# First norm of a two-layer trunk: gain and bias as columns behind the transposition, and the square root at both ends on ScalarE

## The chip, the cores and the metric

The kernel runs on one core of a Trainium2 chip. The metric is the device time of one execution in microseconds (us); lower is better. TensorE (PE) multiplies matrices, VectorE (DVE), ScalarE (ACT) and GpSimd (POOL) work elementwise, and SyncE (SP) issues nearly all transfers. The engines run their own streams and meet at semaphores.

## The reference

The input is 256 tokens of width 1024 in float32. It is normalised first, and then two layers follow, each a mixer and a feed-forward part, each with a residual and another norm. Only the first and the last norm are touched by the change.

```
def _layer_norm(x, g, b):
    mu = mean(x, -1); var = mean((x - mu)**2, -1)
    return (x - mu) * rsqrt(var + 1e-5) * g + b

x = _layer_norm(x, ln_in_g, ln_in_b)
for l in range(2):
    mix = mixer(x, w_in[l], ...)          # starts with x @ w_in[l], 1024 x 6662
    x = _layer_norm(alpha * x + mix, ln1_g[l], ln1_b[l])
    ffn = swiglu(x, w_gate[l], w_up[l], w_down[l])
    x = _layer_norm(alpha * x + ffn, ln2_g[l], ln2_b[l])
```

## The kernel before

The 256 tokens are two tiles of 128 rows, `x[0]` and `x[1]`, of eight blocks of 128 columns each. `write_plan` writes one list of steps, and every engine walks it and does its own part of each step, so the order on an engine is the order of the list.

Weights arrive in pieces of up to 128x2048 in three `raw` buffers. ScalarE copies each to `w_hi` (step `hi`), VectorE subtracts to get `w_lo` (step `lo`), and TensorE multiplies in three products (L1438). SyncE may load the next piece into a `raw` buffer when the `lo` step of its last content is done.

The very first 512 columns of `w_in` go another way, since they need no splitting. They come in four quarters (`first_raw`, two blocks of rows each) and are multiplied in plain float32 (step `first_mm`, L1418: two records of TensorE for each product). The start runs so:

- TensorE works on zeros first (step `warm`, L1386), then spreads gain and bias, loaded as four rows, over all partitions of four banks (`spread_rows`, L1396), then does three more `warm` products.
- VectorE takes the statistics of a tile (L1317, L1319). GpSimd raises variance + 1e-5 to the power -0.5 (L946). VectorE corrects that root by one Newton step (L1337, L1340), and applies mean, gain, root and bias to `x` (L1327, L1347, L1350).
- TensorE transposes the blocks of `x` into a bank (step `turn_rows`, L1408), ScalarE copies the bank to `merged` (L1084), and TensorE multiplies that with `first_raw`. Later ScalarE and VectorE split `merged` into the two parts that all later pieces use (step `split_rows`, L1089, L1360).
- When tile 0 has its 512 columns, ScalarE copies the bank to `stages` (L1013), and TensorE transposes that (`turn_qk`, L1491) between the second and the third quarter of tile 1. Then come the pieces of the split kind (L1438).

At the end VectorE sums the last bank into `x` (L1278), ScalarE squares (L1094), GpSimd makes the root in two instructions (L953, L955), VectorE corrects it and scales (L1298, L1301, L1366), and SyncE stores the result.

## Time and profile before

| | |
|---|---|
| median of 3 runs | 831.04 us (830.87 to 831.71) |
| the profiled execution's own time | 831.25 us |
| its span in the profile | 829.5 us |
| TensorE busy | 819.2 us (99%) |
| VectorE, ScalarE, GpSimd busy | 535.7 us (65%), 435.9 us (53%), 55.4 us (7%) |
| chain that ended last | TensorE 95% |

The span runs from the first to the last recorded instruction; the execution's own time holds 1.75 us around it. Busy shares are means over the whole span, and the change touches the first 50 us and the last 10 us, so those stretches are read by themselves.

### The profile page before, as it was taken

Reading aid. Unit: us, or ns where it says so; the run is one execution under the profiler, and the core shown is the slowest. Engines: PE = TensorE matmul, PEld = TensorE weight load, DVE = VectorE, ACT = ScalarE, POOL = GpSimd, SP = SyncE. Lnnn points to the kernel's source line nnn. Section 1 sums busy time; section 2 is a strip of 40 time slices with the busy share of each in tenths; the row PEclk is TensorE's granted clock in tenths of the full one; section 3 lists DMA queues with packets and bytes.
Section 4 is the critical chain, followed back from the end, with each engine's and each line's share of the span. In section 5 each row is a group of like instructions: output and inputs, shape, how many; then the busy total and the mean of one; then the engine's idle time right before and its main releaser. Section 6 shows DMA issues by size and latency. Waiting matters only on the chain.

```text
span 829.5 us, 11237 instructions
## 1 busy us (share of the span) xinstructions
PE 819.2 (99%) x4305; PEld 684.4 (83%) x4305; DVE 535.7 (65%) x783; ACT 435.9 (53%) x622; POOL 55.4 (7%) x105
## 2 busy tenths in 40 slices
PE   9999999999999999999999999999999999999996
PEld 5888888888888888888889788878888888888885
DVE  7655656475776667566767656564686767576764
ACT  4667767654455344434448667666445544435431
POOL 0022230000000000000000414100000000000000
PEclk9999999999999999999999999999999999999999
DMA  8854443566448655654437543437754675656401
GB/s 296 273 192 140 140 141 127 179 227 216 139 152 303 206 185 171 216 190 152 153 110 251 177 151 113 144 103 250 243 190 149 207 252 165 224 169 202 169 37 51
DMA packets 93500, 148.33 MB, mean 179 GB/s; under 512 B 3460, under 2 KB 54916, under 8 KB 93448
## 3 DMA queue, kind: packets, MB, share of 16 engines
q1 hardware_dynamic: 93448, 147.62, 54.2%
q8 instruction: 35, 0.57, 0.3%
q14 instruction: 17, 0.14, 0.0%
HBM read 146.56 MB, written 1.05 MB: 178 GB/s over the span
## 4 chain that ended last, share of the span: by engine, by line
PE 95%; DVE 1%; DMA 1%; issue 1%; ACT 1%; SPq 1%; POOL 0%; POOLq 0%; DVEq 0%; ACTq 0%
PE bank L1438 62%; PE bank L1464 16%; PE bank L1467 8%; PE bank L1572 1%; PE bank L1562 1%; PE bank L1550 1%; PE bank L1481 1%; DMA raw<-in_w_in 1%; PE bank L1526 1%; PE bank L1491 1%; PE bank L1418 1%; DVE w_lo L1137 0%; DVE x L1278 0%; SPq L855 0%; SPq L851 0%
## 5 line engine op out<-in xcount | busy, mean ns | idle before, releaser
L1137 DVE TENSOR_TENSOR w_lo<-raw,w_hi 128x2048 fp32r<-128x2048 f32 (+5 forms) x182 | 310.1, 1714 | 94.3 <-ACT w_hi L990 93.9
L1438 PE MATMUL bank<-w_hi,act_parts 128*128 128x512 f32 (+2 forms) x1120 | 349.9, 384 | 0.7 <-DVE w_lo L1137 0.6
L990 ACT CAST w_hi<-raw 128x2048 fp32r<-128x2048 f32 (+3 forms) x140 | 253.5, 1812 | 104.9 <-PE bank L1467 56.8
L1438 PEld LDWEIGHTS bank<-w_hi,act_parts 128*128 128x128 f32 x1120 | 207.6, 188 | 39.7 <-issue 3.0
L1438 PE MATMUL bank<-w_lo,act_parts 128*128 128x512 f32 (+2 forms) x560 | 211.4, 378 | 0.0
L1464 PE MATMUL bank<-act_parts,w_hi 128*128 128x512 f32 x576 | 140.4, 391 | 0.0
L1464 PEld LDWEIGHTS bank<-act_parts,w_hi 128*128 128x128 f32 x576 | 105.7, 188 | 20.4
L1438 PEld LDWEIGHTS bank<-w_lo,act_parts 128*128 128x128 f32 x560 | 105.4, 188 | 16.9 <-issue 0.2
L1438 PE MATMUL bank<-w_hi,y_hi 128*128 128x512 f32 x240 | 94.9, 395 | 0.0
L1438 PE MATMUL bank<-w_lo,y_hi 128*128 128x512 f32 x240 | 93.6, 390 | 0.0
L1438 PE MATMUL bank<-w_hi,y_lo 128*128 128x512 f32 x240 | 93.5, 390 | 0.0
L1255 DVE TENSOR_REDUCE act_fns<-bank 128x256 f32<-128x512 f32 x72 | 47.9, 686 | 50.0 <-PE bank L1464 49.8
L1467 PEld LDWEIGHTS bank<-act_parts,w_lo 128*128 128x128 f32 x576 | 76.2, 191 | 4.2
L1467 PE MATMUL bank<-act_parts,w_lo 128*128 128x256 f32 x576 | 77.5, 282 | 0.0
L1438 PEld LDWEIGHTS bank<-w_hi,y_lo 128*128 128x128 f32 x240 | 45.0, 188 | 9.7
L1438 PEld LDWEIGHTS bank<-w_hi,y_hi 128*128 128x128 f32 x240 | 45.1, 188 | 9.1 <-issue 0.3
L1438 PEld LDWEIGHTS bank<-w_lo,y_hi 128*128 128x128 f32 x240 | 45.2, 188 | 8.4
L1105 ACT ACTIVATE act_fns<-act_fns 128x256 f32<-128x256 f32 x36 | 15.1, 418 | 70.2 <-DVE act_fns L1255 70.2
L1049 ACT ACTIVATE shared<-shared,neg_max 128x128 f32<-128x128 f32 (+3 forms) x64 | 33.7, 528 | 18.7 <-DVE neg_max L1206 13.4
L953 POOL TENSOR_SCALAR var_eps<-square_sum 128x1 f32<-128x1 f32 x8 | 1.5, 191 | 584.2 <-ACT prob_t_squares L1094 584.2
L1068 ACT ACTIVATE shared<-shared,rdenom 128x128 f32<-128x128 f32 (+1 forms) x64 | 25.6, 448 | 27.7 <-DVE rdenom L1226 27.7
L1152 DVE TENSOR_TENSOR qk_parts<-bank,qk_parts 128x512 fp32r<-128x512 f32 (+1 forms) x24 | 14.4, 600 | 32.4 <-ACT qk_parts L1019 32.4
(135 smaller groups left out, 564.7 us busy)
## 6 DMA issues: line engine op xcount, KB each, us to landing
raw<-in_w_in SPq DMA_DIRECT2D x42, 1024.0 KB, 5.1
raw<-in_w_gate SPq DMA_DIRECT2D x44, 512.0 KB, 4.0
raw<-in_w_up SPq DMA_DIRECT2D x44, 512.0 KB, 5.1
raw<-in_w_down SPq DMA_DIRECT2D x22, 1024.0 KB, 4.9
raw<-in_w_o SPq DMA_DIRECT2D x8, 1024.0 KB, 5.1
raw<-in_w_in SPq DMA_DIRECT2D x8, 768.0 KB, 4.6
raw<-in_w_pa SPq DMA_DIRECT2D x4, 768.0 KB, 4.5
raw<-in_w_pc SPq DMA_DIRECT2D x4, 768.0 KB, 4.5
```

Source lines behind the costliest of these rows:

```text
L990: act.copy(weights(w_hi, i, HI_SLOTS), weights(raw, i, RAW_SLOTS)).then_inc(hi_done, 1)
L1049: act.activation(pr, pr, ACT.Exp, bias=neg_max[:, slot:slot + 1], scale=-1.0, accum_out=denom[:, slot:slot + 1]).then_inc(exp_done, 1)
L1068: ins = act.activation(pr, pr, ACT.Identity, scale=rdenom[:, slot:slot + 1])
L1105: act.activation(a[:, 0:256], a[:, 0:256], ACT.Silu).then_inc(silu_done, 1)
L1137: dve.tensor_tensor(weights(w_lo, i, HI_SLOTS)[:, cols], weights(raw, i, RAW_SLOTS)[:, cols], weights(w_hi, i, HI_SLOTS)[:, cols].bitcast( ...
L1152: dve.tensor_tensor(qk_lo[ev["g"] % 2][:, pairs, cols], group_view(bank[b], ev["np"], P), qk_hi[ev["g"] % 2][:, pairs, cols].bitcast(F32), ...
L1255: dve.tensor_reduce(a[:, part * SEQ:(part + 1) * SEQ], bank[b][:, :].rearrange("p (h n) -> p n h", h=2), mybir.AxisListType.X, ALU.add).th ...
L1418: ins = pe.matmul(bank[use[0]][:, :], merged[t][:, at_k * P:(at_k + 1) * P], first_raw[q][:, k, :], start=at_k == 0, stop=at_k == KT - 1)
L1438: ins = pe.matmul(bank[use[0]][:, 0:width], a, w[:, k, c0:c0 + width], start=start and k == 0 and p == 0, stop=stop and k == nk - 1 and p ...
L1464: ins = pe.matmul(out[:, :], wh[:, k, cols], act_parts[:, at_k, :, :], start=begins and k == 0, stop=ends and k == 3)
L1467: ins = pe.matmul(out[:, 0:SEQ], wl[:, k, cols], hi["act"][:, at_k, :], start=begins and k == 0, stop=ends and k == 3)
L1481: ins = pe.transpose(out[:, k * P:(k + 1) * P], source(src, buf, k0 + k, t), ident)
```

## The change

Gain and bias of the first norm are loaded as 2 x 8 columns beside the identity matrix (`FIRST_COLS`), so that after the transposition, where the channels lie on the partitions, ScalarE puts them on as scale and bias of its copy out of the bank. One instruction of 128 columns for each block takes the place of one for a whole bank. VectorE only subtracts the mean and multiplies by the root. `spread_rows` goes away, and TensorE's work on zeros becomes 20 products in one go. The first half of `x[0]` and the identity are loaded from ScalarE's queue. The first and the second block of tile 0 have a bank each, and TensorE multiplies the first before it transposes the third and fourth. The root of tile 0 is ScalarE's `Abs_reciprocal_sqrt`. Since the rows of `x` now lack gain and bias, both are loaded to all partitions later, and GpSimd completes the rows (`complete_rows`) before the first scores. In the last norm ScalarE makes the root itself. The pieces of the diff stand in the order plan, SyncE, GpSimd, ScalarE, VectorE.

```
-WARM = (10, 3)
+WARM = 20
...
-    plan.append(("warm", WARM[0]))
-    plan.append(("spread_rows", spread_rows))
-    plan.append(("warm", WARM[1]))
-    plan.append(("first_norm", 0, spread_rows))
-    turn_rows(0, (0, 2), (2, 2))
-    plan.append(("first_norm", 1, spread_rows))
+    plan.append(("warm", WARM))
+    plan.append(("first_norm", 0))
+    turn_rows(0, (0, 1), (1, 1, bank(1)))
+    plan.append(("first_norm", 1))
...
-            first_mm(0, 0, use0[0])
+            first_mm(0, 0, use0[0], (0,))
+            turn_rows(0, (2, 2))
+            first_mm(0, 0, use0[0], (1,))
             turn_rows(0, (4, 4))
             split_rows(0)
             first_mm(0, 1, use0[0])
-            split_hi()
             first_mm(0, 2, use0[0])
             turn_rows(1, (0, 4))
+            split_hi()
             first_mm(0, 3, use0[0])
...
+                    if (layer, c, half, t) == (0, 2, 1, 0):
+                        plan.append(("complete_rows",))
...
-            sp.dma_start(norm_rows, d["norms"]).then_inc(norms_loaded, 16)
-            load_x(0)
+            load_x(0, 1)
             load_first(0)
-            sp.dma_start(tables[:, 0:P], d["tables"][:, 0:P]).then_inc(ident_loaded, 16)
             load_first(1)
-            load_x(1)
+            load_x(1, 0, 1)
...
+                    if i == 2 * RAW_SLOTS - 1:
+                        sp.wait_ge(filled[first_chunk[0]], first_chunk[1])
+                        broadcast_gain_bias(0)
...
+                elif step[0] == "complete_rows":
+                    pool.wait_ge(gb_loaded, 32)
+                    for t in range(TT):
+                        for b, n in first_turns[t]:
+                            pool.wait_ge(drained[b], n)
+                        link(pool.tensor_tensor(x[t][:, :], x[t][:, :], gain_bias[:, 0, :], ALU.mult))
+                        pool.tensor_tensor(x[t][:, :], x[t][:, :], gain_bias[:, 1, :], ALU.add).then_inc(rows_complete, 1)
...
+            act.dma_start(x[0][:, 0:NW], d["x"][0:P, 0:NW]).then_inc(x_loaded[0][0], 16)
+            act.dma_start(tables[:, 0:FIRST_COLS], d["norms"]).then_inc(ident_loaded, 16)
...
+                elif kind == "first_norm" and step[1] == 0:
+                    act.wait_ge(eps_ready, 1)
+                    link(act.activation(early_root[:, :], eps[:, :], ACT.Abs_reciprocal_sqrt))
+                    act.wait_ge(first_var, 1)
+                    act.activation(rstd[:, 0:1], mean_var[:, 0, 1:2], ACT.Abs_reciprocal_sqrt,
+                                   bias=eps[:, :]).then_inc(first_root, 1)
...
-                    act.copy(merged[t][:, k0 * P:(k0 + nk) * P], bank[b][:, 0:nk * P]).then_inc(drained[b], 1)
+                    for k in range(nk):
+                        at_k = k0 + k
+                        ins = act.activation(merged[t][:, at_k * P:(at_k + 1) * P], bank[b][:, k * P:(k + 1) * P],
+                                             ACT.Identity, scale=gain_cols[:, at_k:at_k + 1],
+                                             bias=bias_cols[:, at_k:at_k + 1])
+                    ins.then_inc(drained[b], 1)
...
+                        if step[3] == 2 * DEPTH:
+                            act.wait_ge(squares_ready, means)
+                            act.activation(rstd[:, t:t + 1], square_sum[:, t:t + 1], ACT.Abs_reciprocal_sqrt, bias=eps[:, :],
+                                           scale=1.0 / D_MODEL).then_inc(root_ready, 1)
...
+                    if u["u"] == 0:
+                        dve.wait_ge(rows_complete, TT)
...
+                    def normalise(c0, c1):
+                        return dve.tensor_scalar(x[t][:, c0:c1], x[t][:, c0:c1], mean_var[:, t, 0:1], rstd[:, one],
+                                                 ALU.subtract, ALU.mult)
```

The order of instructions shows the change at three places. First, ScalarE's stream at the start of the kernel, before; `merged` is the transposed tile, `act_parts` its split form, `w_hi` a weight piece, `stages` the first 512 columns of tile 0, and the brackets hold the semaphores waited for.

```order
L1084 ACT_TABLE_LOAD
L1084 COPY merged<-bank 128x256 [waits filled7]
L1084 COPY merged<-bank 128x256 [waits filled6]
L1084 COPY merged<-bank 128x512 [waits filled7]
L1089 CAST act_parts<-merged 128x8x128 [waits drained7,drained6]
L990 CAST w_hi<-raw 128x1536 [waits raw_full0]
L1084 COPY merged<-bank 128x512 [waits filled6]
L1084 COPY merged<-bank 128x512 [waits filled7]
L990 CAST w_hi<-raw 128x1536 [waits raw_full1]
L1013 COPY stages<-bank 128x512 [waits filled0]
L1089 CAST act_parts<-merged 128x8x128 [waits drained7,drained6]
```

The same place in the changed kernel, from its first copies out of a bank to the copy to `stages`:

```order
L1110 ACTIVATE merged<-bank,tables 128x128 [waits ident_loaded,filled6]
L1110 ACTIVATE merged<-bank,tables 128x128
L1110 ACTIVATE merged<-bank,tables 128x128 [waits ident_loaded,filled7]
L1110 ACTIVATE merged<-bank,tables 128x128 x3
L1118 CAST act_parts<-merged 128x8x128 [waits drained6,drained7,drained1]
L1110 ACTIVATE merged<-bank,tables 128x128 [waits ident_loaded,filled6]
L1110 ACTIVATE merged<-bank,tables 128x128 x3
L1007 CAST w_hi<-raw 128x1536 [waits raw_full0]
L1110 ACTIVATE merged<-bank,tables 128x128 [waits ident_loaded,filled7]
L1110 ACTIVATE merged<-bank,tables 128x128 x3
L1007 CAST w_hi<-raw 128x1536 [waits raw_full1]
L1030 COPY stages<-bank 128x512 [waits filled0]
```

Each copy of 512 columns has become four of 128, and the first weight piece has moved from ahead of both copies of tile 1 to between them; the copy to `stages` still stands behind two weight pieces and both sets of copies of tile 1.

Second, TensorE's stream before the first split pieces, before; `tables` holds the identity, `shared` and `act_fns` the quarters of the first weights:

```order
L1386 MATMUL bank<-logf_lo,logf_hi 128x256 [waits ident_loaded]
L1386 MATMUL bank<-logf_lo,logf_hi 128x256 x2
L1408 MATMUL bank<-tables,x 128x128 [waits first_quarter]
L1408 MATMUL bank<-tables,x 128x128
L1408 MATMUL bank<-tables,x 128x128 [waits x_ready]
L1408 MATMUL bank<-tables,x 128x128
L1418 MATMUL bank<-shared,merged 128x512 [waits first_loaded0,drained7]
L1418 MATMUL bank<-shared,merged 128x512
L1408 MATMUL bank<-tables,x 128x128 [waits drained7,x_ready]
```

And the same place now, from its very start:

```order
L1405 MATMUL bank<-logf_lo,logf_hi 128x256 [waits logf_zeroed]
L1405 MATMUL bank<-logf_lo,logf_hi 128x256 x19
L1416 MATMUL bank<-tables,x 128x128 [waits first_quarter,ident_loaded] x2
L1426 MATMUL bank<-shared,merged 128x512 [waits drained7,first_loaded0]
L1416 MATMUL bank<-tables,x 128x128 [waits x_ready,ident_loaded]
L1416 MATMUL bank<-tables,x 128x128
L1426 MATMUL bank<-shared,merged 128x512 [waits drained1,first_loaded0]
L1416 MATMUL bank<-tables,x 128x128 [waits drained7,x_ready,ident_loaded]
L1416 MATMUL bank<-tables,x 128x128 x3
```

The eight products that spread gain and bias are gone, the work on zeros stands in one go ahead of everything, and the first product needs only the first block.

Third, ScalarE's last instructions, before and then now; `rstd` is the root, `prob_t_squares` the squares:

```order
L1105 ACTIVATE act_fns<-act_fns 128x256 [waits drained6]
L1107 CAST y_hi<-act_fns 128x256 [waits hid_done]
L1094 ACTIVATE prob_t_squares,square_sum<-x,neg_mean 128x1024 [waits mean_ready] x2
```

```order
L1138 ACTIVATE act_fns<-act_fns 128x256 [waits drained6]
L1140 CAST y_hi<-act_fns 128x256 [waits hid_done]
L1143 ACT_TABLE_LOAD
L1143 ACTIVATE early_root<-eps 128x1 [waits eps_ready]
L1123 ACTIVATE prob_t_squares,square_sum<-x,neg_mean 128x1024 [waits mean_ready,act_own]
L1127 ACTIVATE rstd<-square_sum,eps 128x1 [waits squares_ready]
L1123 ACTIVATE prob_t_squares,square_sum<-x,neg_mean 128x1024 [waits mean_ready]
L1127 ACTIVATE rstd<-square_sum,eps 128x1 [waits squares_ready]
```

A table load and a root on a constant have come behind the last feed-forward copy, and each square is followed by the root.

## Rows read from the trace of the kernel before

**Rows 1.** Chain of waits, 0 to 30 us: start us, us, what.
```profile
0.72 0.37 SPq L857
...
1.15 0.36 SPq L851
...
17.45 3.70 PE bank L1418 x8
21.15 0.44 PE bank L1491 x4
21.59 3.44 PE bank L1418 x8
25.02 4.19 PE bank L1438 x24
```

**Rows 2.** Stretches: us, busy time of each engine, TensorE clock, DMA share, GB/s.
```profile
8.70:24.40 15.70, 15.40 (x47) 7.59 (x48) 13.27 (x20) 9.53 (x13) 0.55 (x1) 1.00 0.98 337
24.40:820.00 795.60, 794.82 (x4227) 670.06 (x4226) 511.12 (x736) 423.46 (x607) 52.78 (x94) 1.00 0.54 177
```

**Rows 3.** Timeline of TensorE, 0 to 26 us.
```profile
1.33 2.50 PE L1386 MATMUL bank<-logf_lo,logf_hi 128*128 128x256 f32 x10 [1.33 <-POOL logf_lo L916]
...
6.83 0.63 PE L1396 MATMUL bank<-w_lo,w_hi 128*128 128x512 f32 x1
7.39 0.70 PE L1386 MATMUL bank<-logf_lo,logf_hi 128*128 128x256 f32 x3
...
8.77 1.98 PE L1418 MATMUL bank<-shared,merged 128*128 128x512 f32 x4 [0.24 <-ACT merged L1084]
```

**Rows 4.** Timeline of VectorE, 0 to 22 us.
```profile
4.03 1.34 DVE L1317 BATCH_NORM_STATS2 stats<-x 128x6 f32<-128x512 f32 x2 [0.47 <-DMA x<-in_x]
5.40 0.21 DVE L1319 BATCH_NORM_AGGREGATE mean_var<-stats 128x2 f32<-128x12 f32 x1
...
6.64 0.22 DVE L1337 SCALAR_TENSOR_TENSOR newton<-rstd,half_var 128x1 f32<-128x1 f32 x1
6.89 0.16 DVE L1340 SCALAR_TENSOR_TENSOR rstd<-newton,rstd 128x1 f32<-128x1 f32 x1
7.09 0.48 DVE L1347 SCALAR_TENSOR_TENSOR x<-x,rstd,bank 128x256 f32<-128x256 f32 x1
```

**Rows 5.** Timeline of ScalarE, 0 to 22 us.
```profile
15.44 1.47 ACT L990 CAST w_hi<-raw 128x1536 fp32r<-128x1536 f32 x1 [2.46 <-DMA raw<-in_w_in]
16.82 1.07 ACT L1084 COPY merged<-bank 128x512 f32<-128x512 f32 x2
17.77 1.48 ACT L990 CAST w_hi<-raw 128x1536 fp32r<-128x1536 f32 x1
19.14 0.60 ACT L1013 COPY stages<-bank 128x512 f32<-128x512 f32 x1
```

**Rows 6.** Groups of ScalarE by form: count, busy us, mean ns, idle before.
```profile
L1068 ACT ACTIVATE shared<-shared,rdenom 128x128 f32<-128x128 f32 x32 | 11.1, 395 | 19.1 <-DVE rdenom L1226 19.1
...
L1028 ACT ACT_TABLE_LOAD x1 | 1.3, 1283 | 0.0
...
L1013 ACT COPY values<-bank 128x128 f32<-128x128 f32 x4 | 1.1, 286 | 0.0
...
L1028 ACT ACTIVATE f_exp<-f_neg_abs 128x12 f32<-128x12 f32 x2 | 0.4, 212 | 0.6 <-DVE f_neg_abs L1163 0.6
```

**Rows 7.** Timeline of ScalarE, 52 to 66 us.
```profile
59.98 0.69 ACT L1068 ACTIVATE shared<-shared,rdenom 128x128 f32<-128x128 f32 x2 [1.97 <-DVE rdenom L1226]
```

**Rows 8.** Timeline of the end, GpSimd, then VectorE, 820 to 829.5 us.
```profile
824.18 0.19 POOL L953 TENSOR_SCALAR var_eps<-square_sum 128x1 f32<-128x1 f32 x1 [7.33 <-ACT prob_t_squares L1094]
...
825.11 0.22 DVE L1298 SCALAR_TENSOR_TENSOR newton<-rstd,half_var 128x1 f32<-128x1 f32 x1 [0.77 <-POOL rstd L955]
```

**Rows 9.** Groups of GpSimd by form.
```profile
L963 POOL TENSOR_TENSOR shared<-shared 128x512 f32<-128x512 f32 x4 | 6.9, 1726 | 0.3
```

**Rows 10.** Timeline of VectorE, 51 to 55 us.
```profile
53.52 0.49 DVE L1191 TENSOR_TENSOR shared<-bank,tables 128x128 f32<-128x128 f32 x2
```

More of the change, by code:

```diff
@@ L277, in turn_rows @@
     def turn_rows(t, *parts):
-        for k0, nk in parts:
-            use = aux_bank()
+        for k0, nk, *other in parts:
+            use = other[0] if other else aux_bank()
             turned.update({("first", t, k): use for k in range(k0, k0 + nk)})
@@ L826, in group_view @@
             return ap[:, 0:groups * width].rearrange("p (g k) -> p g k", g=groups)
+        first_chunk = next(step[3] for step in PLAN if step[0] == "first_mm" and step[1:3] == (TT - 1, QUARTERS - 1))
         first_turns = [[step[4] for step in PLAN if step[0] == "turn_rows" and step[1] == t] for t in range(TT)]
@@ L947, in _ @@
                                        ALU.pow).then_inc(first_root, 1)
-                elif step[0] == "statistics":
+                elif step[0] == "statistics" and step[3] < 2 * DEPTH:
                     for t, _ in step[1]:
@@ L1107, in _ @@
                     act.copy(hi["y"][:, 2 * (c % 3) + j, :], a[:, 256:512]).then_inc(hid_hi_done, 1)
+                    if turned_n == last_turned:
+                        act.wait_ge(eps_ready, 1)
+                        link(act.activation(early_root[:, :], eps[:, :], ACT.Abs_reciprocal_sqrt))
         @block.vector
@@ new lines, in _ @@
+                    if t:
+                        link(dve.bn_aggr(mean_var[:, t, :], stats[:, t, :, :]))
+                        dve.tensor_scalar(var_eps[:, one], mean_var[:, t, 1:2], LN_EPS, None,
+                                          ALU.add).then_inc(first_var, 1)
+                    else:
+                        dve.bn_aggr(mean_var[:, t, :], stats[:, t, :, :]).then_inc(first_var, 1)
+                        dve.wait_ge(first_var, 1)
+                    link(dve.tensor_scalar(half_var[:, one], mean_var[:, t, 1:2], LN_EPS, -0.5, ALU.add, ALU.mult))
@@ L1387, in _ @@
                                   start=True, stop=True)
-                elif kind == "spread_rows":
-                    pe.wait_ge(rows_hi_done, 1)
-                    pe.wait_ge(rows_lo_done, 1)
-                    for a, uses in enumerate(step[1]):
-                        for j, use in enumerate(uses):
-                            out, done = take(use)
-                            r = 2 * a + j
-                            for p, part in enumerate((rows_hi, rows_lo)):
-                                ins = pe.matmul(out[:, :], row_pick[:, r:r + 1].broadcast_to([P, P]), part,
-                                                start=p == 0, stop=p == 1)
-                            ins.then_inc(done, 1)
-                    pe.wait_ge(ident_loaded, 16)
                 elif kind == "turn_rows":
                     _, t, k0, nk, use = step
-                    if (t, k0) == (0, 0):
+                    pe.wait_ge(ident_loaded, 16)
+                    if t == 0 and k0 < 2:
                         pe.wait_ge(first_quarter, 1)
@@ L1410, in _ @@
                 elif kind == "first_mm":
-                    _, t, q, use, (b, n) = step
-                    pe.wait_ge(drained[b], n)
+                    _, t, q, use, rows = step
                     pe.wait_ge(first_loaded[q], 16)
-                    if q == 0:
-                        take(use)
-                    for k in range(2):
+                    for k in rows:
                         at_k = 2 * q + k
+                        if at_k == 0:
+                            take(use)
+                        pe.wait_ge(drained[rows[k][0]], rows[k][1])
                         ins = pe.matmul(bank[use[0]][:, :], merged[t][:, at_k * P:(at_k + 1) * P],
```

111 lines of the change are left out of this document (40 added, 71 removed).

## The prediction

> **What bounds the kernel now.** I read the busy time by stretches first. From 24.4 to 820 us TensorE is busy 794.82 of 795.60 us [rows 2], so nothing on the other engines is worth anything there unless it makes TensorE wait. From 8.7 to 24.4 us it is busy 15.40 of 15.70 us, but before 8.77 us it only works on zeros, spreads gain and bias and transposes [rows 3]. So the time is: when TensorE begins useful work, plus fixed work, plus its gaps up to 25 us, plus the tail behind its last product. The change can act in the first and the last of these, and in the gaps.
>
> In the chain of waits the point to watch is where the first split piece begins, at 25.02 us [rows 1]: from there on the stream is unchanged. Ahead of it stand the transposition of the first result (21.15 us) and four products of two records, 3.44 us, so one costs 0.86 us; four transposes cost 0.44 us.
>
> **The start, up to the first product.** VectorE begins the statistics at 4.03 us, having waited for the transfer of `x` [rows 4], which was issued at 1.15 us behind the four rows of gain and bias [rows 1]. Now both halves are issued at about 0.72 us from two queues. The first half alone would come 0.4 us sooner; but the two now share the transfer engines, and the statistics before ran over both halves in one go (1.34 us for two), so the second half was no wait. Bounds: 0.3 us sooner to 0.2 us later. I take no change. The aggregate ends at 5.61 us.
>
> ScalarE's root has no row. The nearest is a ScalarE instruction on 12 columns, 0.212 us; an operand read for each partition adds 0.395 - 0.286 = 0.11 us at 128 columns [rows 6]; so 0.32 us, from 5.66 to 5.98. Newton begins at 6.03 instead of 6.64 us; its two steps take 0.25 and 0.20 us [rows 4], and the first 256 columns begin at 6.48 us. They took 0.48 us with a second tensor; without it, between half of the streaming part saved (0.34) and nothing (0.48); I take 0.40: 6.88 us against 7.57. One block's transposition I put at 0.4 us with its pipeline (four take 0.44), one copy with scale and bias at 0.50 us (0.395 with one such operand, 0.11 for the second), wakes 0.1 us: the first product begins at 7.9 us instead of 8.77 [rows 3], some **0.85 us sooner**.
>
> **From the first product to the split pieces.** This is where I expect the gain to go. ScalarE now puts four instructions where one was. Two of 128 columns with one operand for each partition took 0.69 us together, 0.395 each alone, so they follow each other at 0.295 us [rows 6, 7]; with a second such operand 0.295 to 0.40 us. I take 0.39, for the second operand is read like the first. A bank then takes 3 x 0.39 + 0.49 = 1.66 us; before it was about 0.6, and two banks 1.07 us [rows 5]. At 0.295 it is 1.28 us.
>
> TensorE: product, two transposes, product, four transposes: 7.9 + 0.1 + 0.86 + 0.22 + 0.86 + 0.44 = 10.4 us. Two products end at 12.1 us; blocks 4 to 7 reach `merged` at 10.6 + 1.66 = 12.25, a wait of 0.15 us. Two more products, 14.0 us; transposes of tile 1, 14.45 us, in the bank at 14.6 us. Then product pairs, transposes and the first half of tile 1 bring TensorE to the transposition of `stages` at about 20.2 us by the chain's count, 0.95 us ahead of before (it also loses the gap it had before 17.45 us).
>
> ScalarE's stream decides whether `stages` is there. Before: piece 0 at 15.44 us, waiting for its transfer, both copies at 16.82, piece 1 at 17.77, `stages` from 19.14 to 19.74 us [rows 5]: 1.4 us before TensorE's 21.15. Now the four copies of tile 1 begin at 14.65, and piece 0 follows them at 16.2 us, no longer bound by its transfer. Then 1.38 us to the next copies, 4 x 0.39 = 1.56, piece 1 and 1.37 us, `stages` 0.60: 21.1 us. TensorE's transposition follows some 0.3 us later (wake, weights, pipeline), at 21.4 us instead of the 20.2 it could. The split pieces begin 0.44 + 3.44 us later, at 25.3 us, against 25.02: **0.3 us lost**, though the first product came 0.85 us sooner. With 0.295 us for each copy every number falls: copies from 14.45, piece 0 at 15.65, `stages` at 20.15, split pieces at 24.35: 0.7 us won. With 0.40 us it is 0.4 lost. These are the bounds of the term.
>
> The Trainium skill bears on this: "ScalarE: Activation LUTs", What ACT_TABLE_LOAD costs, says that each operand read for each partition adds some 93 ns and that instructions in a row overlap by as much. By its figures two operands give 0.386 us from one to the next, and the term would be the 0.3 us lost that I take; if the second operand is free, it would be 0.7 us won. The rows agree for one operand (0.295); none has two.
>
> **What else is added, and its cover.** The root needs a different activation table, so a load of 1.283 us [rows 6] comes before the exponential of the forget gate; the instruction waited 0.6 us for VectorE there, so the chain slips 0.7 us. It feeds a sum that TensorE reaches some 4 us after its input is ready, and ScalarE's next piece is not needed for several us: nothing. Gain and bias for all partitions are 1 MB more behind the sixth piece; at the 337 GB/s of rows 2 that is 3.1 us on the pieces behind. They are copied near 35 us and multiplied after 50 us: nothing, as long as the delay stays below about 8 us. GpSimd's four passes of 1024 columns: the nearest row is 512 columns in 1.726 us [rows 9], so up to 3.5 us each, 14 us, from about 35 to 49 us. VectorE waits for them in front of the first scores, at 53.52 us [rows 10]: hidden by 4 us. If that cover were gone, each us beyond would stop VectorE, the splits queued behind it, and then TensorE.
>
> **The end.** GpSimd wakes at 824.18 us, and VectorE gets the root at 825.11 us, having been idle 0.77 us [rows 8]. Now ScalarE goes on itself at about 824.2 us and takes 0.32 us; VectorE at 824.55 us: **0.55 us won** (0.45 to 0.65). The table load before it falls on an idle ScalarE.
>
> **Sum.** 0.3 us lost at the start, 0.55 won at the end: 0.25 us won, 831.25 to 831.0 us for the profiled execution. That execution lies 0.21 us over the median of the runs shown, 831.04, so I expect 830.8 us.
>
> **Rivals.**
> *A, the copies are cheap.* The second operand costs nothing; split pieces 0.7 us sooner, with the end 1.25 us: 829.8 us. With `x` 0.3 us sooner too, and a quick subtraction, 829.3. For it: scale and bias may be fetched together. Against it: the first operand cost 0.11 us.
> *B, TensorE's clock is still low at the first product* (the other side). Ten products of 256 columns took 2.50 us from 1.33 us on, three took 0.70 us at 7.39 us, and the products between, to 6.83 us, run at the slow pace too [rows 3]: the 1.2 GHz level held until about 7.4 us of nearly unbroken work, and it was at 2.4 GHz in time for 8.77 us. Now 20 products of about 0.22 us end at 5.8 us, and TensorE idles until 6.95 us. If the rise then comes at 11 us, half of 7.9 to 11 us is lost, 1.55 us, and slower transposes 0.1: 832.4 us. A rise at 13 us gives 833.4. From the point where the rise is later than about 8.5 us it cancels the gain. The Trainium skill, "TensorE: Matmul & The Clock Gate", The HAM clock gate, says that the low level is the default, that sustained activity ends it, and that the moment varies between executions of one kernel. By that rule some executions rise during the 20 products and some do not; one trace cannot show it.
> *C, the completed rows come late.* If a pass on GpSimd took over 4.6 us, the first scores would wait; at 6 us each that is 5.5 us on VectorE, of which perhaps 2 reach TensorE: 832.8 us or more. The rows give 3.5 us at most.
>
> **How the numbers follow.** The main case (830.3 to 831.4 us) gets 0.42, A 0.24, B 0.28, C 0.06. About 0.2%, 1.7 us, is what a measurement of this kernel can tell from no change: 829.4 to 832.7 us. A reaches below it with 0.15; B beyond it with 0.10 and C with 0.03. So faster 0.15, same 0.72, slower 0.13. The range leaves out the far ends of A and of B and C, 0.1 each: 829.2 to 832.8 us.
>
> **What the profile after would show.** The first product at 7.9 us and at most 0.5 us for one copy; four copies in 1.66 us (1.28 in A); TensorE waiting about 1.2 us for `stages` ahead of its transposition; the split pieces at 25.3 us; work on zeros and first products at either pace, which tells B; the first scores not waiting for GpSimd; VectorE's last correction waiting some 0.2 us for the root instead of 0.77. A start of the statistics more than 0.3 us from 4.03 us, or a wait of TensorE for weights behind 30 us, would show a step that I have not priced.

## The result and the profile after

The change made the kernel slower: 839.24 us median of 5 runs (838.25 to 840.04), against 830.87 us for the kernel before on the same chip (830.81 to 831.71). The ratio is 1.0096, with a 95% interval of 1.0085 to 1.0107. The profiled execution took 840.04 us with a span of 838.2 us, 8.7 us more than the span before.

The stretches of the kernel after stand below (us, busy time of each engine, granted TensorE clock, DMA share, GB/s):

```profile
8.70:25.50 16.80, 16.18 (x47) 7.86 (x46) 8.57 (x14) 12.13 (x22) 0.56 (x1) 0.90 0.72 244
25.50:60.00 34.50, 30.18 (x158) 26.66 (x157) 23.99 (x20) 21.19 (x30) 15.46 (x7) 0.91 0.71 243
60.00:820.00 760.00, 759.35 (x4031) 637.97 (x4030) 490.21 (x707) 404.14 (x578) 51.20 (x90) 1.00 0.54 175
```

From 60 us on TensorE is as full as in [rows 2]. Ahead of that it idles for 4.3 us between 25.5 and 60 us, where before it did not idle at all, and in both early stretches the mean clock is below full. TensorE's five longest waits in the kernel after (line, releaser: us in total, times, longest) name the place:

```profile
PE bank L1509 <- DVE logf_lo L1209: 4.3, 1, 4.3
PE bank L1416 <- DVE x L1358: 1.5, 1, 1.5
PE bank L1405 <- POOL logf_lo L921: 1.3, 1, 1.3
PE bank L1499 <- ACT stages L1030: 0.6, 1, 0.6
PE bank L1426 <- ACT merged L1110: 0.5, 1, 0.5
```

L1509 is the running sum of the forget gate's logarithms, a product of TensorE that needs VectorE's last result of the gate (`logf_lo`). GpSimd's timeline of the kernel after from 36 us on (start us, us) shows the four passes:

```profile
36.95 4.36 POOL L954 TENSOR_TENSOR x<-x,shared 128x1024 f32<-128x1024 f32 x1 [26.44 <-DVE qk_parts L1188]
41.38 2.40 POOL L955 TENSOR_TENSOR x<-x,shared 128x1024 f32<-128x1024 f32 x1
43.74 4.44 POOL L954 TENSOR_TENSOR x<-x,shared 128x1024 f32<-128x1024 f32 x1
48.26 3.22 POOL L955 TENSOR_TENSOR x<-x,shared 128x1024 f32<-128x1024 f32 x1
```

VectorE's timeline of the same stretch shows what it did beside them:

```profile
36.76 2.28 DVE L1173 TENSOR_TENSOR w_lo<-raw,w_hi 128x2048 fp32r<-128x2048 f32 x1
41.46 4.47 DVE L1173 TENSOR_TENSOR w_lo<-raw,w_hi 128x2048 fp32r<-128x2048 f32 x1 [2.42 <-ACT w_hi L1007]
45.85 0.41 DVE L1188 TENSOR_TENSOR qk_parts<-bank,qk_parts 128x256 fp32r<-128x256 f32 x1
46.19 3.08 DVE L1173 TENSOR_TENSOR w_lo<-raw,w_hi 128x1024 fp32r<-128x1024 f32 x1
49.19 2.33 DVE L1196 TENSOR_TENSOR f_in<-f_in,f_bias 128x12 f32<-128x12 f32 x1
51.55 0.17 DVE L1199 SCALAR_TENSOR_TENSOR f_neg_abs<-f_in 128x12 f32<-128x12 f32 x1
...
54.26 0.21 DVE L1209 TENSOR_TENSOR logf_lo<-neg_logf,logf_hi 128x48 fp32r<-128x48 f32 x1 [0.35 <-ACT logf_hi L1054]
```

The same subtraction of 2048 columns takes 2.28 us where it begins ahead of GpSimd's first pass, and 4.47 us beside a pass. An addition on 12 columns takes 2.33 us and ends at 51.52 us, just behind GpSimd's last pass (51.48 us). So `logf_lo` starts at 54.26 us, where before it started at 43.63 us.

Laid side by side, the two timelines look as if one engine stood while the other worked. The second pass ends at 43.78 us, and the subtraction begun at 41.46 us ends 2.15 us later; the third pass ends 2.25 us behind that, the subtraction of 1024 columns 1.09 us behind that, the fourth pass 2.21 us behind that, and the small addition 0.04 us behind the pass. Undisturbed, they take 2.29 us (subtraction), 2.40 us (the second pass), 1.22 us and 0.16 us. The first pass fits as well: it stood behind the subtraction begun at 36.76 us. The operation on `qk_parts`, which reads one of its two inputs out of a bank, took 0.41 us while the third pass ran, as in the kernel before (0.43 us).

The clock follows. These are slices of 2 us of the kernel after, with the same columns as above:

```profile
52.00:54.00 2.00, 0.00 (x0) 0.00 (x0) 0.35 (x2) 1.99 (x6) 0.00 (x0) 0.89 0.00 0
54.00:56.00 2.00, 1.48 (x5) 1.48 (x6) 1.34 (x2) 2.00 (x4) 0.00 (x0) 0.50 0.00 0
56.00:58.00 2.00, 2.00 (x6) 1.52 (x6) 1.87 (x1) 2.00 (x3) 0.00 (x0) 0.50 0.56 116
58.00:60.00 2.00, 2.00 (x6) 1.54 (x5) 1.93 (x4) 1.97 (x3) 1.08 (x3) 0.50 1.06 397
60.00:62.00 2.00, 2.00 (x16) 1.39 (x15) 1.97 (x2) 0.00 (x0) 2.00 (x1) 0.90 1.02 363
```

TensorE had been idle since 50.2 us; it resumes at 54.52 us at 1.2 GHz, does 6 records in a slice (56 to 60 us) where at 2.4 GHz it does 11 of this kind (42 to 48 us), and gets the full clock back just behind 60 us. Half of its busy time in the three slices at 0.50 and a tenth of the last are lost, 2.9 us. The Trainium skill, "TensorE: Matmul & The Clock Gate", HAM oscillation, says that idle gaps between bursts of products bring the low level back; these slices agree.

At the start the same happens once more. TensorE's timeline of the kernel after:

```profile
1.33 4.61 PE L1405 MATMUL bank<-logf_lo,logf_hi 128*128 128x256 f32 x20 [1.33 <-POOL logf_lo L921]
7.43 0.41 PE L1416 MATMUL bank<-tables,x 128*128 128x128 f32 x2 [1.50 <-DVE x L1358]
8.37 1.24 PE L1426 MATMUL bank<-shared,merged 128*128 128x512 f32 x2 [0.53 <-ACT merged L1110]
9.41 0.64 PE L1416 MATMUL bank<-tables,x 128*128 128x128 f32 x2
9.84 1.91 PE L1426 MATMUL bank<-shared,merged 128*128 128x512 f32 x2
```

ScalarE's timeline of the kernel after, with its root and the first pair of the new copies:

```profile
6.01 0.29 ACT L1102 ACTIVATE rstd<-mean_var,eps 128x1 f32<-128x1 f32 x1 [2.87 <-DVE mean_var L1353]
7.77 0.81 ACT L1110 ACTIVATE merged<-bank,tables 128x128 f32<-128x128 f32 x2 [1.47 <-PE bank L1416]
```

And VectorE's, which begins 0.35 us later than in [rows 4]:

```profile
4.38 1.29 DVE L1346 BATCH_NORM_STATS2 stats<-x 128x6 f32<-128x512 f32 x2 [4.38 <-DMA x<-in_x]
```

The first product's two records take 1.24 us, the second product's 1.91 us, although both have the same shape: the clock fell between them, behind the idle time from 5.94 to 7.43 us. The mean granted clock from 9.0 to 12.6 us was 0.53.

So the first split piece starts at 26.42 us instead of 24.46 us by TensorE's records (1.96 us). With 4.32 us of idle time and 2.9 us of low clock, less 0.57 us won at the end (shown below), this is 8.6 of the 8.7 us.

### The profile page after: what moved, and what is told of

The parts are those of the page before. It is cut to its first block, busy times and chain, and to the rows that moved or that the text cites. A ratio compares the mean times of both kernels' runs of the same rounds, so it can differ in the third digit from the quotient of the medians.

```text
span 838.2 us, 11253 instructions
## 1 busy us (share of the span) xinstructions
PE 822.2 (98%) x4304; PEld 686.3 (82%) x4304; DVE 536.3 (64%) x772; ACT 443.1 (53%) x640; POOL 68.1 (8%) x105
## 4 chain that ended last, share of the span: by engine, by line
PE 91%; DVE 3%; DMA 3%; ACT 2%; issue 1%; SPq 0%; POOL 0%; DVEq 0%; ACTq 0%
PE bank L1446 59%; PE bank L1472 16%; PE bank L1475 8%; PE bank L1580 1%; DVE w_lo L1173 1%; DMA raw<-in_w_in 1%; PE bank L1570 1%; PE bank L1426 1%; PE bank L1558 1%; PE bank L1534 1%; PE bank L1489 1%; PE bank L1499 1%; DMA raw<-in_w_up 1%; DMA x<-in_x 0%; ACT w_hi L1007 0%
## 5 line engine op out<-in xcount | busy, mean ns | idle before, releaser
L1173 DVE TENSOR_TENSOR w_lo<-raw,w_hi 128x2048 fp32r<-128x2048 f32 (+5 forms) x182 | 314.3, 1736 | 100.3 <-ACT w_hi L1007 100.0
L1188 DVE TENSOR_TENSOR qk_parts<-bank,qk_parts 128x512 fp32r<-128x512 f32 (+1 forms) x24 | 14.4, 600 | 29.5 <-ACT qk_parts L1036 29.5
```

Source lines behind the costliest of these rows:

```text
L1173: dve.tensor_tensor(weights(w_lo, i, HI_SLOTS)[:, cols], weights(raw, i, RAW_SLOTS)[:, cols], weights(w_hi, i, HI_SLOTS)[:, cols].bitcast( ...
L1188: dve.tensor_tensor(qk_lo[ev["g"] % 2][:, pairs, cols], group_view(bank[b], ev["np"], P), qk_hi[ev["g"] % 2][:, pairs, cols].bitcast(F32), ...
```

## The experiments

All medians are in us, beside runs of the kernel before on the same chip. The edits are cut to the lines that matter and moved to the left; `...` marks lines left out.

### The end alone

```
+if step[3] == 2 * DEPTH:                      # ScalarE, last norm, on the kernel before
+    act.wait_ge(squares_ready, means)
+    act.activation(rstd[:, t:t + 1], square_sum[:, t:t + 1], ACT.Abs_reciprocal_sqrt,
+                   bias=eps[:, :], scale=1.0 / D_MODEL).then_inc(root_ready, 1)
...
```

The table for this root is loaded early, as in the change, and GpSimd's two instructions for the last norm are left out.

> The kernel before, with one part of the change alone: the root of the last row tile's last norm is taken by ScalarE from its own sum of squares, its table loaded early. The prediction priced this at 0.55 us won. Compared with the kernel before (830.9): 830.3, ratio 0.9993 to 0.9994, and in the profile the Newton step waits some 0.2 us for ScalarE instead of 0.77 us for GpSimd. If the rest of the span between the profiles (8.7 us longer) hid a loss in the end too, this would be at or over the time of before.

Measured: 830.49 (11 runs) against 831.03 (27 runs), ratio 0.9993 (0.9984 to 1.0002). The medians differ by 0.54, as forecast, though the interval includes 1. The profile shows the step itself. VectorE's timeline at the end of this kernel:

```profile
824.33 0.22 DVE L1310 SCALAR_TENSOR_TENSOR newton<-rstd,half_var 128x1 f32<-128x1 f32 x1 [0.19 <-ACT rstd L1103]
```

The same place in the kernel after:

```profile
833.94 0.22 DVE L1336 SCALAR_TENSOR_TENSOR newton<-rstd,half_var 128x1 f32<-128x1 f32 x1 [0.20 <-ACT rstd L1127]
```

The wait is 0.19 us instead of 0.77 [rows 8]. This part works.

### Passes and loads taken out

```
-link(pool.tensor_tensor(x[t][:, :], x[t][:, :], gain_bias[:, 0, :], ALU.mult))
-pool.tensor_tensor(x[t][:, :], x[t][:, :], gain_bias[:, 1, :], ALU.add).then_inc(rows_complete, 1)
+pool.memset(pass_mark[:, t:t + 1], 0.0).then_inc(rows_complete, 1)
...
```

> The changed kernel with GpSimd's four passes (gain, then bias, on both row tiles, 128x1024 each) left out, so gain and bias are missing in the rows that the residual adds; the two broadcasts of gain and bias and SyncE's wait ahead of them stay. Theory 1, GpSimd's passes hold VectorE (its 2048 column subtraction took 4.47 instead of 2.29 us, a 128x12 addition 2.33 instead of 0.16), the forget gate's sum comes 4.3 us late and the idle TensorE loses its clock: 4.3 + 3.4 = 7.7 us come back, 831.5 (830.5 to 832.5), and no low clock behind 50 us. Theory 2, the broadcasts and the wait in SyncE's queue hold up the pieces (the casts waited 3.28, 2.62 and 0.90 us for them): 837 or more. Between the two (833 to 836): the 4.3 us come back and the clock stays low for another reason.

Measured: 832.72 (10 runs, 830.81 to 833.17), ratio 1.0017 (1.0008 to 1.0027). Removing four GpSimd instructions brings back 6.5 of the 8.4 us. The median is just above the range I gave (830.5 to 832.5): in the profile the clock at the start is low here too (below), and TensorE waits 0.9 us for `cum_row`, VectorE's next result of the gate. Transfers and SyncE's wait are untouched here, so by themselves they are not where the time went. No run has the passes without the loads in the changed kernel, so how much of the 6.5 us needs both is not shown.

```
-sp.wait_ge(filled[first_chunk[0]], first_chunk[1])
-broadcast_gain_bias(0)
...
```

> As the one before it, and without the two broadcasts for the first norm and SyncE's wait for the last first product too; the later norms' gain and bias are loaded as before. Theory 1: the transfers are covered, same time as with them within 0.3 us (about 831.5). Theory 2: all of the loss but the start's comes back only here, 831 to 832 while the kernel with the transfers stays at 837 or more. If both kernels gain a part, the difference of the two is the price of the transfers.

Measured: 832.45 (10 runs, 830.97 to 833.70), ratio 1.0015 (1.0006 to 1.0024): without the passes the broadcasts cost 0.3 us by the medians, which runs that spread over 2.4 and 2.7 us do not tell from nothing. But they are not without effect. `logf_lo` is ready at 45.25 us without them and at 48.80 us with them, and TensorE comes for it at 48.38 and 49.74 us. The spare time is 3.1 us without the broadcasts, 0.9 us with them (these two profiled runs differ in the start's clock as well, see below), and it was 4.2 us in the kernel before (43.84 to 48.09 us).

The runs fall in two groups: three without loads lie at 830.97 to 831.11, seven at 832.26 to 833.70. The profiled one was among the three. Its first stretches:

```profile
9.00:12.60 3.60, 3.60 (x14) 1.56 (x11) 2.30 (x8) 2.31 (x6) 0.56 (x1) 1.00 1.05 387
12.60:25.50 12.90, 12.29 (x39) 6.09 (x39) 7.68 (x7) 10.72 (x17) 0.20 (x2) 1.00 0.72 231
```

The first of them in the profiled run of the kernel with the loads, which took 832.79 us:

```profile
9.00:12.60 3.60, 3.60 (x12) 1.78 (x11) 2.29 (x8) 1.05 (x3) 0.56 (x1) 0.69 1.05 387
```

The clock at the start differs, 1.00 against 0.69, and the two groups of the kernel without loads lie 1.6 us apart (medians 831.07 and 832.67). Each run's mean granted clock goes the same way in the kernel without loads: 0.998 in the three quick runs, 0.995 to 0.997 in the seven others. Where in the run the clock was low is read from one profile of each kind; the next runs test it.

### TensorE kept at work until the transposition

```
-WARM = 20
+WARM = 28
```

> The changed kernel with 28 warm-up products instead of 20, so that TensorE is at work until the first transpositions instead of idle from 5.94 to 7.43 us. Theory 3: that idle stretch is what takes the clock down between 9.19 and 12.6 us, and half of this stretch is lost by it: 1.7 us come back, 837.5 (837.0 to 838.2). Rival: the low stretch comes from the chain of short transpositions and products behind 7.43 us (each waits for a copy), which stay: 839.2, within 0.3 us of the changed kernel, with the clock low at 9 to 12 us as before. A third way: the warm-up ends too late and holds the transpositions up, 839.5 or more.

Measured: 836.66 (5 runs, 836.36 to 837.39), ratio 1.0069 (1.0056 to 1.0082), 2.6 us better than the kernel after. TensorE now idles 0.3 us ahead of its transposition, and the clock from 9 to 12.6 us is 1.00. I had forecast 1.7 us (837.0 to 838.2), too little: the first split piece came 1.33 us sooner (25.09 us), and the wait for `logf_lo` fell from 4.3 to 3.4 us as well.

To test the two groups, the same was done to the kernel without passes and loads:

> The changed kernel without passes, broadcasts and SyncE's wait (gain and bias are missing in the rows that the residual adds), with 28 warm-up products. It is what the prediction summed: start, copies, end. Theory 3, the start's clock is what keeps the kernel without passes and loads at 832.5 in 7 of 10 executions and lets it at 831.0 in 3: all executions at 830.6 to 831.2. If the low executions stay (832.4 and more), the idle time ahead of the transpositions is not what lowers the clock. The prediction's own sum, 830.8, should be met within 0.3.

Measured: 830.95 (11 runs, 830.77 to 831.22), ratio 0.9995 (0.9986 to 1.0003). The group above 832 us is gone in all 11 runs. With 8 more products on zeros, this kernel holds the terms that my sum counted (start, copies, end) and of those that it put at nothing only the table load, and it comes within 0.15 us of the 830.8 forecast.

### The passes alone, in the kernel before

Nothing else of the change is in this kernel; the passes work on the gate's buffers, which are idle then, and neither on `x` nor on the loaded gain and bias. ScalarE waits for their end before it writes there.

```
+elif step[0] == "idle_passes":                # GpSimd, on the kernel before
...
+    pool.wait_ge(hi_done, 6)
+    for op in (ALU.mult, ALU.add, ALU.mult, ALU.add):
+        link(pool.tensor_tensor(act_fns[:, 0:1024], act_fns[:, 0:1024], act_fns[:, 1024:2048], op))
...
```

> The kernel before with GpSimd's four passes of 128x1024 and two inputs added to it alone, on idle memory (the gate's buffers, which nobody reads until they are overwritten), from some 34 us on; no other part of the change. The same output is computed. Theory 1 (GpSimd's passes hold VectorE wherever VectorE subtracts beside them): the 2048 column subtraction behind 34 us takes 3.5 to 4.5 instead of 2.29 us, the forget gate's last VectorE result comes 3 to 7 us later than 43.63, and since TensorE wants it only at 48.0, 0 to 3 us are lost; with the clock falling in addition up to 5: 831.0 to 836, likeliest 832.5. Rival: it is the changed kernel's later start and later pieces alone that made the passes dear; then 831.0 and subtractions of 2.29 us.

Measured: 836.45 (5 runs, 836.11 to 836.53), ratio 1.0061 (1.0048 to 1.0075): 5.3 us lost by four instructions on an engine that is 7% busy, and above the range that I gave (831.0 to 836). GpSimd's timeline in this kernel:

```profile
33.85 14.56 POOL L952 TENSOR_TENSOR act_fns<-act_fns 128x1024 f32<-128x1024 f32 x4 [21.56 <-ACT w_hi L1001]
```

VectorE's beside it:

```profile
34.76 8.06 DVE L1149 TENSOR_TENSOR w_lo<-raw,w_hi 128x2048 fp32r<-128x2048 f32 x2
...
43.08 3.09 DVE L1149 TENSOR_TENSOR w_lo<-raw,w_hi 128x1024 fp32r<-128x1024 f32 x1
46.09 2.35 DVE L1172 TENSOR_TENSOR f_in<-f_in,f_bias 128x12 f32<-128x12 f32 x1
48.48 0.17 DVE L1175 SCALAR_TENSOR_TENSOR f_neg_abs<-f_in 128x12 f32<-128x12 f32 x1
```

And TensorE's, where it waits for the forget gate:

```profile
51.45 0.59 PE L1513 MATMUL bank<-upper_r,logf_hi 128*128 128x384 f32 x1 [3.25 <-DVE logf_lo L1185]
```

Two subtractions take 8.06 us (before: 4.48 us), and `f_neg_abs` starts 7.55 us later than before (40.93 us). Less the 4.2 us of spare time, that is 3.35 us, near TensorE's wait of 3.25 us. The clock is 0.50 from 52 to 54 us and 0.75 from 54 to 56 us, which costs 1.5 us more. The rival, that only the late start made the passes dear, falls.

### What in a pass does it

Each pass in four of 256 columns:

```
+for c0 in range(0, D_MODEL, 256):
+    part = slice(c0, c0 + 256)
+    pool.tensor_tensor(x[t][:, part], x[t][:, part], gain_bias[:, 0, part], ALU.mult).then_inc(pool_own, 1)
...
```

> The changed kernel, each of GpSimd's four passes cut into four of 256 columns; the same is computed. Theory 1a, VectorE's instruction is held until GpSimd's present instruction ends (the 128x12 addition took 2.33 us and ended with GpSimd's pass): the small addition is held for a quarter pass at most, 0.2 to 1.1 us, while the 2048 column subtractions are as slow as before, and 1 to 1.5 us of the 8.4 us come back, 837.7 to 838.3. Theory 1b, the two share the memory by halves as long as both have work, so only the sum of the work counts: the small addition is again some 2 us, 839.2 within 0.5. Theory 2 (transfers), already weak: no change.

Measured: 836.25 (4 runs, 835.92 to 838.58), ratio 1.0067 (1.0054 to 1.0081), 3.0 us better than the kernel after. VectorE's timeline:

```profile
43.65 1.68 DVE L1184 TENSOR_TENSOR w_lo<-raw,w_hi 128x1024 fp32r<-128x1024 f32 x1
45.26 0.70 DVE L1207 TENSOR_TENSOR f_in<-f_in,f_bias 128x12 f32<-128x12 f32 x1
45.99 0.65 DVE L1210 SCALAR_TENSOR_TENSOR f_neg_abs<-f_in 128x12 f32<-128x12 f32 x1
...
48.76 0.67 DVE L1215 TENSOR_SCALAR neg_logf<-neg_logf 128x12 f32<-128x12 f32 x1
```

The small addition is held 0.5 us instead of 2.2 us, so it is held for one GpSimd instruction, not for a share of the work. Theory 1b falls. The last line has one input only and is held as well (0.17 us undisturbed). The forecast of 1a (837.7 to 838.3) missed that the big subtractions gain too (1.68 us instead of 3.08 for 1024 columns): now it is the passes that stretch, four quarters to 5.84 us beside VectorE, against 2.82 us where VectorE is mostly idle. TensorE's wait for `logf_lo` shrinks from 4.3 to 0.2 us, but one of 2.1 us for `cum_row` (VectorE's next result of the gate) follows.

The passes with one input:

```
+link(pool.tensor_scalar(x[t][:, :], x[t][:, :], 1.0, None, ALU.mult))
+pool.tensor_scalar(x[t][:, :], x[t][:, :], 0.0, None, ALU.add).then_inc(rows_complete, 1)
```

> The changed kernel with GpSimd's four passes as operations of one input and a constant (times 1, plus 0) in place of two inputs, so gain and bias are missing in the rows that the residual adds. Theory 1, it is the reading of GpSimd's two inputs that holds VectorE: with one input the passes are shorter (under 2 us) and VectorE's subtractions go back to 2.29 us or near, 832 to 834. Rival: any large instruction of GpSimd beside a VectorE instruction of two inputs holds it; then 836 or more, and the subtractions still take over 3 us.

Measured: 834.79 (4 runs, 832.35 to 836.55), ratio 1.0042 (1.0025 to 1.0058). The median lies between the two forecasts, and the runs spread over 4 us; the profiled one is the quickest. In it VectorE is nearly free (one subtraction of 3.01 us, the others 2.29, the small addition 0.17 us), but GpSimd's passes still take 2.8 to 3.7 us. By the medians one input is better than two by 4.45 us. Whether VectorE is released in the slower executions too is not seen.

### The rows completed by VectorE

Except for the one marked below, these kernels compute everything. They have 28 warm-up products, and VectorE makes the two passes over each tile.

```
+def complete_rows(t):                         # VectorE
+    dve.wait_ge(gb_loaded, 32)
+    link(dve.tensor_tensor(x[t][:, :], x[t][:, :], gain_bias[:, 0, :], ALU.mult))
+    link(dve.tensor_tensor(x[t][:, :], x[t][:, :], gain_bias[:, 1, :], ALU.add))
```

> The changed kernel with 28 warm-up products, and with the rows completed by VectorE instead of GpSimd, in its idle time: row tile 0 ahead of the last projection block's subtractions, row tile 1 while ScalarE takes the forget gate's exponential and logarithm (1.88 us idle). Two operations of two inputs and 1024 columns each, 1.22 us by the nearest row (1024 column subtraction), 4.9 us in all against 2.3 + 1.9 us of idle time in these places. Theory 1: TensorE waits for the forget gate's sum no more than 1 us, the clock stays full, 831.0 to 832.3. If the placement of any 5 us of work there costs the clock as well, 835 or more, and the fault would be the completion's place, not its engine.

Measured: 833.89 (5 runs, 833.52 to 835.74), ratio 1.0036 (1.0023 to 1.0049), 1.6 us worse than the upper end I gave, since I had allowed TensorE one wait of up to 1 us, and there were two. TensorE's waits in this kernel:

```profile
PE bank L1536 <- DVE cum_row L1219: 1.6, 1, 1.6
PE bank L1407 <- POOL logf_lo L921: 1.3, 1, 1.3
PE bank L1511 <- DVE logf_lo L1213: 1.3, 1, 1.3
```

The clock stays at 1.00 throughout, in spite of these two waits. An operation takes 1.22 us here, against 2.40 to 4.44 us on GpSimd.

```
+elif kind == "turn_rows" and step[1:3] == (1, 4):   # VectorE instead of ScalarE
...
+        ins = dve.tensor_scalar(merged[t][:, at_k * P:(at_k + 1) * P],
+                                bank[b][:, (at_k - k0) * P:(at_k - k0 + 1) * P],
+                                gain_cols[:, at_k:at_k + 1], bias_cols[:, at_k:at_k + 1],
+                                ALU.mult, ALU.add)
```

> As the one before it, and the last four transposed blocks of row tile 1 are put on by VectorE (gain as multiplier, bias as addend, from the bank) instead of ScalarE's four copies of 0.39 us. The prediction's step: ScalarE's copies make the stages late, 0.3 us lost against before. If right, TensorE's wait of 0.6 us for the stages goes and this kernel is 0.5 to 0.7 us faster than the one before it, 830.4 to 831.7. If the stages are held by something else than the copies (the cast of the weights ahead of them), the two are equal within 0.2 us.

Measured: 833.24 (11 runs, 832.42 to 835.67), ratio 1.0029 (1.0020 to 1.0039), 0.65 us better than the one before it, as forecast, but above the range I gave (830.4 to 831.7), since the two waits for the gate stay (0.9 and 1.6 us). The runs of the two kernels overlap. Without passes and loads, so with gain and bias missing in the rows that the residual adds, the same edit gives the clean comparison:

> As the one before it (no passes, no broadcasts, 28 warm-up products; gain and bias missing in the residual's rows), with the last four transposed blocks of row tile 1 put on by VectorE. The prediction's term of 0.3 us lost by ScalarE's copies: TensorE's wait of 0.6 us for the stages goes, 829.9 to 830.4. If it isn't the copies, 830.8 as without them.

Measured: 830.24 (11 runs, 830.11 to 830.43), ratio 0.9988 (0.9980 to 0.9997), 0.71 us below the 830.95 of the kernel with ScalarE's copies, and no run of one lies among those of the other. VectorE's four take 1.37 us, and TensorE's wait for `stages` is gone.

Last, with everything computed again, row tile 0 is completed one step earlier in the order, in VectorE's wait for a cast:

```
-if (layer, c, half, t) == (0, 2, 1, 0):
+if (layer, c, half, t) == (0, 2, 0, TT - 1):
```

> The version with the rows completed by VectorE and the shared copies (833.2), with row tile 0's completion moved ahead of the 2048 column subtraction at 38.8 us, into the 2.1 us that VectorE waits there for ScalarE's cast; row tile 1's stays in the wait for the exponential and logarithm. All is computed. Of TensorE's waits for the forget gate's sum and its row (0.9 + 1.6 us) 2.1 us should go: 831.1, range 830.5 to 832.0. If the broadcasts land too late for this place (behind 37 us), the subtraction behind it comes later and it stays at 832.5 or more.

Measured: 830.98 (11 runs, 830.41 to 831.70), ratio 0.9997 (0.9989 to 1.0006), where I had forecast 831.1. VectorE's timeline:

```profile
36.48 1.22 DVE L1163 TENSOR_TENSOR x<-x,shared 128x1024 f32<-128x1024 f32 x1
37.73 1.23 DVE L1164 TENSOR_TENSOR x<-x,shared 128x1024 f32<-128x1024 f32 x1
39.05 2.29 DVE L1175 TENSOR_TENSOR w_lo<-raw,w_hi 128x2048 fp32r<-128x2048 f32 x1
```

Both passes fit into the idle time, and the subtraction starts only 0.3 us later than in the version that completed tile 0 behind it (38.77 us). This computes the whole reference, is 8.3 us faster than the kernel after and cannot be told from the kernel before. No version that computes everything beat the kernel before by more than the measurement can tell; the best of them is the end alone, 830.49. Only the incomplete kernel with shared copies has an interval below 1. In the last kernel TensorE still waits 0.7 us for `cum_row`.

## Why the prediction was wrong

I forecast 830.8 us (829.2 to 832.8) and gave slower by over 0.2% a chance of 0.13. It took 839.24 us.

**The step that failed** is the one on GpSimd: "up to 3.5 us each, 14 us, from about 35 to 49 us ... hidden by 4 us". The size came out nearly right by luck: four passes, 14.4 us, from 36.95 to 51.48 us. But a pass that was not held up took 2.40 us; the three others stretched to 3.22 to 4.44 us because they too stood behind VectorE. VectorE's first scores never waited for them. What failed is that I priced them only by who waits for their result. I did not ask whose instructions they run beside. The passes held three of VectorE's instructions up by 2.2, 1.9 and 2.2 us (4.47 for 2.29, 3.08 for 1.22, 2.33 for 0.16), the forget gate came 5.7 us later than without them (54.26 against 48.59 us), and TensorE idled 4.3 us and then ran 2.9 us short at 1.2 GHz. In the kernel before the passes alone cost 5.3 us, in the kernel after 6.5 us by the medians with and without them. With the passes out, the median is 832.72 us, inside the stated range; they alone took the kernel out of it. My rival C had the right instructions and the wrong mechanism: it let them be late, and asked for 4.6 us each.

The profile before had a row that warned of it. It stands in GpSimd's timeline there, beside VectorE's subtraction of 51.20 to 53.49 us:

```profile
51.72 2.09 POOL L937 TENSOR_TENSOR rope_cos<-stages,tables 128x128 f32<-128x128 f32 x1 [39.33 <-ACT stages L1013]
53.89 0.46 POOL L938 TENSOR_TENSOR rope_sin<-stages,tables 128x128 f32<-128x128 f32 x1
```

Two instructions of one shape: 2.09 us beside a two-input subtraction, 0.46 us when it has ended. Here GpSimd is the one that is held; with a large GpSimd instruction ahead it is VectorE. The Trainium skill, "GPSIMD Engine Reference", Specifications, states that GpSimd shares its memory interfaces with VectorE and that they contend where VectorE's instruction has two inputs in that memory. By that rule VectorE's subtractions for `w_lo`, which have two such inputs, were all suspects. The trace of before agrees, and so do the subtractions and the additions held beside passes with two inputs, and `qk_parts`, with one of its inputs in a bank, which was not held. The passes with one input mostly left the subtractions alone in the one profile, and an instruction of VectorE with one input was held beside quartered passes; the sentence on two inputs decides neither.

**The second failed step** is in rival B, which I gave 0.28: the place and the price were right, the reading was not. I took the clock to be low at first ("the 1.2 GHz level held until about 7.4 us"). The rows do not say so. This is the stretch from 0 to 9 us of the kernel before, with the clock behind the busy times, and two of its products that spread gain and bias:

```profile
0.00:9.00 9.00, 7.42 (x26) 5.82 (x27) 6.74 (x16) 1.93 (x3) 1.34 (x8) 1.00 0.68 219
4.70 0.63 PE L1396 MATMUL bank<-w_hi 128*128 128x512 f32 x1
5.12 0.63 PE L1396 MATMUL bank<-w_lo,w_hi 128*128 128x512 f32 x1
```

The granted clock is 1.00, and the products of 512 columns start some 0.43 us apart, as they do at full clock later (eight in 3.44 us). My mean of 0.25 us for ten products held the slow first record: in the kernel after the first of 20 took 0.58 us and the rest followed at 0.21 us. There, too, the clock was full until 9.2 us, and fell behind the idle 1.5 us. So nothing rose late; idle time took the level away. That costs 1.6 us (the two groups of runs). With 8 more products on zeros the clock from 9 to 12.6 us is 1.00 in every profile, and the 11 runs of the kernel without passes and loads lie within 0.45 us.

**"Nothing" for the loads** held for the time (0.3 us by the medians, without the passes) and failed for the cover: with SyncE's wait they used 2.2 of the 3.1 us of spare time at the forget gate. I gave the loads and the passes a cover each, and both drew on the same one, VectorE's lead at the forget gate. **The table load** was over-priced: I let the exponential slip by 0.7 us, but ScalarE loaded the table while it waited for VectorE. Without passes and loads the load ran from 41.24 us, VectorE's result was ready at 42.42 us and the exponential began at 42.54 us. What took the spare time from 4.2 to 3.1 us there was a later piece: ScalarE's cast of it began at 38.37 us, having waited 1.38 us for the transfer, where before it began at 37.04 us.

**Steps that held.** ScalarE's root took 0.29 us (forecast 0.32); from the statistics to Newton it is 2.04 us (2.00); four copies 1.50 us (1.66), so they follow each other at 0.34 us, between the two bounds (0.295 and 0.40). The split pieces at full clock start at 24.77 us with 20 products on zeros and at 24.90 us with 28, instead of 24.46: 0.31 and 0.44 us lost where I said 0.3. That is luck in part, since two errors nearly cancelled: with 28 products tile 1's copies began at 15.20 us instead of 14.65, and its two sets took 0.16 and 0.13 us less than I had put. Moving four copies to VectorE won 0.71 us, which shows that the copies were what held `stages`. The end won 0.57 us (0.55).

**A term that was mis-sized.** The statistics began at 4.38 us, 0.35 us later than in [rows 4]; I had allowed 0.2. The transfer of the first half took 3.64 us. With this, and 0.1 us more on the way, the first product came at 8.37 us, 0.40 us sooner instead of 0.85.

## What to carry to other kernels

An instruction moved to an idle engine is priced twice: by who waits for its result, and by what runs beside it. For GpSimd, read off the trace what VectorE does in that time, and whether two of its instructions of one shape already differ there. Cover is a single purse: add up all that draws on one stretch of spare time before calling any of it hidden. And where TensorE is the bound, an idle stretch can cost itself and a low clock behind it; here eight products on zeros were worth 1.5 us without the passes and 2.6 us with them.

## What the runs showed of the hardware that was not expected

- An addition of 12 columns on VectorE took 2.33 us beside a GpSimd pass of 1024 columns, 0.70 us beside passes of 256 and 0.17 us beside none; it ends with the GpSimd instruction. In the other direction a GpSimd pass of 1024 columns took 4.36 us where it began just behind a VectorE subtraction of 2048 columns, and 2.40 us where it began just ahead of one.
- TensorE resumed at 2.4 GHz behind waits of 1.3 and 1.6 us between full stretches (the first version completed by VectorE), and at 1.2 GHz behind 3.3, 3.4 and 4.3 us. In the kernel with the quartered passes it waited 2.1 us, resumed at full clock at 56.05 us and was at 0.50 from 58 to 60 us. At the start, between work on zeros and lone products, the clock fell behind idle stretches of 1.50, 1.53, 1.90 and 2.13 us (the kernel after, quartered passes, no passes, one input) and stayed full behind 1.43 us (no passes and no loads). Ten executions of this last program fall into two groups 1.6 us apart; whether their idle stretches differ or the same stretch is answered in two ways is not shown, for each program has one profile.
